# A feed-forward network in two phases: seven half products for eight in the up-projection, and a down-projection in three rounds summed in PSUM

## The chip, the cores and the metric

The kernel runs on one core of one Trainium2 chip. The metric is the device time of one execution, in microseconds, median of the runs. Matrix products run on TensorE (PE), which reads its stationary operand (128x128, the LDWEIGHTS of the profile) and its moving operand from SBUF and writes PSUM, eight banks of 128x512 fp32. VectorE (DVE), ScalarE (ACT) and GpSimd (POOL) do the elementwise work, SyncE (SP) issues most of the transfers. Each engine works through its own program in order, and the programs wait for each other by semaphores.

## The reference

One inference step of a backbone of two layers, D = 1024, over 128 context tokens and 1024 latent tokens. Each layer is a mixer (layer 0 attention and pooling, layer 1 convolution and a Fourier product), an output projection with a gated residual and LayerNorm, and then the part that changes here, the gated convolutional feed-forward network with 2816 hidden channels:

```python
def conv_ffn(u, w_up, cw, cb, w_down):
    a, g = jnp.split(u @ w_up, 2, axis=-1)
    return (jax.nn.silu(depthwise_conv(a, cw, cb)) * g) @ w_down
...
        u = layer_norm(x) * (1 + sc2) + sh2
        f = conv_ffn(u, w_up[l], ffn_conv_w[l], ffn_conv_b[l], w_down[l])
        x = layer_norm(DEEPNORM_ALPHA * x + g2 * f, ln_g[l, 1], ln_b[l, 1])
```

The convolution runs over three neighbouring tokens, for context and latent tokens apart. Context tokens are modulated and gated by their own vectors.

## The kernel before

The 1152 tokens are nine tiles of 128, tile 0 the context; three tiles make a third of 384 tokens. The 2816 hidden channels are 22 blocks of 128, in 11 groups of two. Every fp32 product is made in three passes: each operand is split into a rounded high part (a copy on ACT, line 905) and the rest, the low part (a subtraction on DVE, line 1434), and PE adds high x high, high x low and low x high.

**Start of the network.** `ln_mid` (line 2030) makes the output projection of the mixer tile by tile. For each tile DVE, POOL and ACT then normalize twice (LayerNorm with gain, then the plain one of the modulation), PE turns the tile (`ln_turn`, transposes into PSUM), ACT modulates it from PSUM and rounds it, and DVE makes its low part. The six chunks of the first hidden block (`first_chunk`) stand between the turns of tiles 6, 7 and 8; a chunk needs the tokens of its own third alone.

**Steady groups.** For a group PE runs four units (two blocks, value and gate) of three chunks (one third each) of 24 matmuls with 384 moving columns (`chunk`, line 2102), 288 in all. ACT copies the value rows out of PSUM, DVE makes the convolution, ACT the SiLU, DVE multiplies by the gate rows in PSUM and splits the product. Then come 108 down matmuls of 512 columns (`down_half`, line 2314): nine tiles, two halves of D, six matmuls each. DVE adds every 128x512 result to a sum in SBUF (line 1747). The residual gate is multiplied into the rows of w_down, twice, since the context has its own. Each weight is loaded and split once.

**End of a layer.** All nine tiles are complete only with the last group. Behind its down matmuls every tile is normalized (ACT, DVE, POOL), and in layer 0 normalized again, turned, modulated and split, with conditioning blocks (`end_block`) and the first Fourier chunks (`four_chunk`) between the turns. In layer 1 the tiles are stored.

## Time and profile before

| | |
|---|---|
| median of three runs | 2805.47 us (2804.4 to 2806.04) |
| span of the profiled execution | 2803.4 us; 2.07 us lie between it and the median of the runs |
| PE busy | 2667.1 us, 95% |
| PE weight loads busy | 2380.4 us, 85% |
| DVE, ACT, POOL busy | 1510.2, 920.3, 422.0 us |
| transfers | 196.09 MB, mean 70 GB/s |

The profile is one execution. A busy share is an average over stretches with different limits, so the views below go stretch by stretch. In a timeline, equal instructions that follow each other stand on one line with their count, and a bracket gives the idle time before the line and what ended it. PEclk is the granted clock of PE, 1.00 being full speed.

### The profile page before, as it was taken

Reading aid. Unit: us, or ns where it says so; the run is one execution under the profiler, and the core shown is the slowest. Engines: PE = TensorE matmul, PEld = TensorE weight load, DVE = VectorE, ACT = ScalarE, POOL = GpSimd, SP = SyncE. Lnnn points to the kernel's source line nnn. Section 1 sums busy time; section 2 is a strip of 40 time slices with the busy share of each in tenths; the row PEclk is TensorE's granted clock in tenths of the full one; section 3 lists DMA queues with packets and bytes.
Section 4 is the critical chain, followed back from the end, with each engine's and each line's share of the span. In section 5 each row is a group of like instructions: output and inputs, shape, how many; then the busy total and the mean of one; then the engine's idle time right before and its main releaser. Section 6 shows DMA issues by size and latency. Waiting matters only on the chain.

```text
span 2803.4 us, 36152 instructions
## 1 busy us (share of the span) xinstructions
PE 2667.1 (95%) x13884; PEld 2380.4 (85%) x13884; DVE 1510.2 (54%) x2157; ACT 920.3 (33%) x1402; POOL 422.0 (15%) x236
## 2 busy tenths in 40 slices
PE   5799899998999999999997999999999999999997
PEld 2487688687999999999995999978899999999995
DVE  2236677656555555555557433356555555555557
ACT  4412677645221222222226411136222222222213
POOL 1060587433000000000007000024000000000003
PEclk7889999999999999999999999999999999999999
DMA  9911100213111111111116212132311111111112
GB/s 330 336 38 36 31 1 1 69 69 136 45 45 37 45 45 39 43 45 45 45 34 257 63 46 67 53 105 87 109 45 45 45 45 45 45 37 40 35 31 83
DMA packets 170992, 196.09 MB, mean 70 GB/s; under 512 B 7098, under 2 KB 125350, under 8 KB 170912
## 3 DMA queue, kind: packets, MB, share of 16 engines
q1 hardware_dynamic: 169844, 194.43, 21.2%
q8 instruction: 53, 0.87, 0.1%
q10 hardware_dynamic: 491, 0.42, 0.1%
q14 instruction: 28, 0.22, 0.0%
q0 software_dynamic: 576, 0.15, 0.0%
HBM read 175.64 MB, written 19.33 MB: 70 GB/s over the span
## 4 chain that ended last, share of the span: by engine, by line
PE 83%; DVE 6%; ACT 4%; issue 3%; DMA 2%; POOL 1%; SPq 0%; ACTq 0%; POOLq 0%; DVEq 0%
PE ps L2106 48%; PE ps L2321 18%; PE ps L2073 5%; DVE small L1634 2%; DMA ada_w<-in_w_ada 2%; PE ps L2056 1%; PE ps L2154 1%; ACT p_exp L1144 1%; PE ps L2212 1%; PE ps L2233 1%; DVE stats L1464 1%; ACT ps L1305 1%; PE ps L2234 1%; PE ps L2018 1%; PE ps L2255 1%
## 5 line engine op out<-in xcount | busy, mean ns | idle before, releaser
L2106 PE MATMUL ps<-act_b,uw 128*128 128x384 f32 x4608 | 807.5, 338 | 8.9 <-DVE act_b L1434 7.4
L2106 PEld LDWEIGHTS ps<-act_b,uw 128*128 128x128 f32 x4608 | 803.6, 189 | 10.7 <-DVE act_b L1434 8.0
L2106 PEld LDWEIGHTS ps<-act_a,uw 128*128 128x128 f32 x3456 | 605.3, 190 | 14.2 <-issue 5.9
L2106 PE MATMUL ps<-act_a,uw 128*128 128x384 f32 x3456 | 610.2, 339 | 6.8 <-DVE act_a L1434 5.3
L2321 PE MATMUL ps<-dw,hh 128*128 128x512 f32 x2112 | 501.4, 397 | 9.1 <-DVE acc L1747 9.1
L2321 PEld LDWEIGHTS ps<-dw,hh 128*128 128x128 f32 x2112 | 397.2, 189 | 111.6 <-DVE acc L1747 9.9
L1747 DVE TENSOR_TENSOR acc<-acc,ps 128x512 f32<-128x512 f32 x360 | 245.8, 686 | 216.7 <-PE ps L2321 216.7
L905 ACT ACTIVATE fa<-ps 128x384 f32<-128x384 f32 (+2 forms) x176 | 67.3, 410 | 839.2 <-PE ps L2106 839.2
L1708 DVE TENSOR_SCALAR ft<-fa,fgrp 128x1153 f32<-128x1153 f32 x44 | 38.7, 880 | 299.0 <-ACT fa L905 284.1
L1434 DVE TENSOR_TENSOR uw<-raw_u,uw 128x1024 fp32r<-128x1024 f32 x112 | 136.6, 1221 | 86.3 <-ACT uw L905 83.0
L849 POOL TENSOR_TENSOR p_low<-p_exp,p_top 128x1536 fp32r<-128x1536 f32 (+1 forms) x50 | 170.9, 3420 | 71.2 <-ACT p_top L905 70.2
L1777 DVE TENSOR_TENSOR fh<-ft,ps 128x384 f32<-128x384 f32 (+2 forms) x176 | 73.9, 450 | 168.4 <-PE ps L2106 160.8
L888 POOL TENSOR_TENSOR acc<-acc,gb_end 128x1024 f32<-128x1024 f32 x9 | 21.3, 2376 | 821.8 <-ACT acc L1285 821.8
L905 ACT ACTIVATE uw<-raw_u 128x1024 fp32r<-128x1024 f32 x112 | 117.8, 1054 | 68.5 <-PE ps L2106 66.2
L905 ACT ACTIVATE hh<-fh 128x384 fp32r<-128x384 f32 x132 | 66.5, 520 | 205.6 <-DVE fh L1777 205.6
L881 POOL TENSOR_SCALAR acc<-acc,stats 128x1024 f32<-128x1024 f32 x9 | 10.8, 1199 | 806.6 <-DVE stats L1472 806.6
L862 POOL TENSOR_TENSOR ln_y<-ln_y,gbm 128x1024 f32<-128x1024 f32 x18 | 43.5, 2417 | 422.9 <-ACT ln_y L985 422.9
L1634 DVE TENSOR_REDUCE small<-ps 128x1 f32<-128x1152 f32 (+1 forms) x72 | 88.7, 1232 | 25.0 <-PE ps L2212 24.3
L1264 ACT ACTIVATE ft<-ft 128x1153 f32<-128x1153 f32 x44 | 51.5, 1171 | 132.7 <-DVE ft L1710 126.8
L1144 ACT ACTIVATE p_exp<-ps 128x1536 f32<-128x1536 f32 (+1 forms) x50 | 71.0, 1421 | 39.4 <-PE ps L2234 39.3
L1639 DVE RECIPROCAL o_inv<-o_raw 64x128 f32<-64x128 f32 x72 | 67.1, 939 | 29.7 <-ACT o_raw L905 28.9
L1434 DVE TENSOR_TENSOR hh<-fh,hh 128x384 fp32r<-128x384 f32 x132 | 73.2, 555 | 17.4 <-ACT hh L905 12.0
(215 smaller groups left out, 3094.2 us busy)
## 6 DMA issues: line engine op xcount, KB each, us to landing
raw_u<-in_w_up SPq DMA_DIRECT2D x88, 512.0 KB, 4.0
ada_w<-in_w_ada SPq DMA_DIRECT2D x52, 512.0 KB, 6.5
raw_d<-in_w_down SPq DMA_DIRECT2D x44, 512.0 KB, 3.7
end_w<-in_w_ada SPq DMA_DIRECT2D x24, 512.0 KB, 7.3
late_w<-in_w_ada SPq DMA_DIRECT2D x20, 512.0 KB, 7.0
raw_u<-in_w_in_odd SPq DMA_DIRECT2D x20, 512.0 KB, 3.9
ln_y<-in_x_all SPq DMA_DIRECT2D x18, 512.0 KB, 4.6
xs<-ln_y SPq DMA_DIRECT2D x18, 512.0 KB, 2.6
```

The lines of the kernel that those rows point to most:

```text
L849: gp.tensor_tensor(p_low[:, s % 3, 0:nb, :], p_exp[:, s % 2, 0:nb, :], p_top[:, s % 3, 0:nb, :].bitcast(F32), ALU.subtract).then_inc(p_lo, 1)
L905: return act.activation(o, i, ACT.Copy)
L1144: act.activation(p_exp[:, s % 2, 0:nb, :], ps[:, 3:3 + nb, :], ACT.Exp).then_inc(exp_done, 1)
L1264: act.activation(ft[:, 1:PADW - 2], ft[:, 1:PADW - 2], ACT.Silu).then_inc(silu_done, 1)
L1434: return v.tensor_tensor(dst, src, hi.bitcast(F32), ALU.subtract)
L1634: v.tensor_reduce(g.peak(h), ps[:, 0:nb, 0:nw], mybir.AxisListType.XY, ALU.max, negate=True).then_inc(mx_done, 1)
L1639: v.reciprocal(o_inv[g.out, cols_], o_raw[g.sum, cols_]).then_inc(inv_done, 1)
L1747: return v.tensor_tensor(a, a, ps[:, 6 + j % 2, :], ALU.add).then_inc(down_added, 1)
L1777: o = v.tensor_tensor(f_h[l][:, s0:s0 + ln], f_t[l][:, p0:p0 + ln], ps[:, 3 + c, s0 - c * CH:s0 - c * CH + ln], ALU.mult)
L2073: mm = pe.matmul(ps[:, 2 * (tile % 3) + h, :], src[:, k, a, tile * P:(tile + 1) * P], wo[l][:, k, w, 512 * h:512 * (h + 1)], start=(k, a, ...
L2106: mm = pe.matmul(out, uw[:, u_slot, w, k, :], src[:, k, a, c * CH:(c + 1) * CH], start=(k, w, a) == (0, 0, 0), stop=(k, w, a) == (KD - 1, ...
L2321: mm = pe.matmul(ps[:, 6 + h, :], hh[l][:, b, a, tile * P:(tile + 1) * P], w_[:, b, w, 512 * h:512 * (h + 1)], start=(b, a, w) == (0, 0, 0 ...
```

## The change

The network of a layer is done in two phases, with the hidden rows kept in DRAM between them.

*Up phase.* The value and the gate rows of a block, over the tokens of the first two thirds and both halves of D, are a product of 2x2 half matrices. It is made from seven half products instead of eight: with weight halves A11, A12 (value) and A21, A22 (gate), DVE forms the sums S1 to S4, and with the tokens of thirds 0 and 1 it forms three sums (`t_ops`) in `split` of tiles 3 to 5. A half product is 12 matmuls of 384 columns. The last third is plain, 48 matmuls. So a block has 132 matmuls instead of 144. Products 2, 3 and 4 are accumulated in PSUM onto 1, 5 and 7, once ACT or DVE has read what these hold; DVE forms the sums (U2, U3, G2, C12, G1) from which the convolution and the gate go on. The high part of a weight or token sum is copied by ACT and its low part made by DVE, ahead of the block that uses it. SP stores the 128x1152 hidden rows of each block.

*Down phase.* Three rounds of three tiles. In a round all 22 rows of w_down (512 KB each) and the matching hidden slices (196 KB) are loaded again and split; each row is 18 matmuls of 512 columns, summed over the 22 rows in PSUM, two banks per tile (`TILE_BANKS`). The last two rows of a round (four in the last) run tile by tile. Splits run ahead of PE by a ring of 3 (first round) or 4. DVE's evacuation of a finished tile (gate, residual), the normalizations, and in layer 0 the turns, modulations and splits of the next layer's tokens are written into the next round, between the splits of its rows j, at the places `run_down` shows. POOL does gain and bias and stores by its own queue. The gate products 3 and 4 move from `ln_mid` to rows 8 and 11 of the first round. After the last round of layer 0 only tiles 6 to 8 are left, beside the Fourier chunks.

*First block.* PE's order there is `first`: product 1, product 5, turn 6, products 7 and 6, turn 7, products 2, 4, 3, turn 8, the plain third. What ACT and DVE do for it stands in `behind(s)`, called between the normalization steps of the last tiles.

Constants and names:

```diff
-END_BANKS = (0, 2, 0, 2, 0, 6, 2, 6, 2)
+B_A, B_D, B_E, B_B, B_F, B_H = range(6)
+KH = KD // 2
+HW = KH * P
+ORDER = ("A11", "A12", "A22", "S2", "S3", "S1", "S4", "A21")
+ORDER0 = ("A11", "A12", "S3", "S1", "S2", "A22", "S4", "A21")
+NI = 3 * NF
+RAWS, RING0, RING1 = 3, 3, 4
+TILE_BANKS = ((6, 7), (0, 1), (2, 3), (4, 5), (6, 7), (0, 1), (2, 3), (4, 5), (6, 7))
+TURN_BANKS = ((2, 3),) * 3 + ((0, 1),) * 6
+FOUR_BANKS = ((2, 3, 4), (5, 6, 7))
+FOUR_ORDER = ((0, 0), (0, 1), (1, 0), (1, 1), (0, 2), (1, 2))
+END_SPOTS = {39: 0, 60: 1}
+END_BANKS = (2, 0, 4, 7, 4, 7)
+LAST_ROWS = 4
```

SyncE:

```diff
+                def down(self, i):
+                    l, (r, f) = self.l, divmod(i, NF)
+                    if i >= RAWS:
+                        sp.wait_ge(dn_lo, NI * l + i - RAWS + 1)
+                    if r == 0:
+                        sp.wait_ge(h_st[f % 2], 16 * (NG * l + f // 2 + 1))
+                    sp.dma_start(d_raw_of(l, i)[:], dram_rows(t["w_down"][l], f)).then_inc(w_ld[i % RAWS], 16)
+                    sp.dma_start(h_raw[i % RAWS][:], h_rows[l][f * P:(f + 1) * P, r * CH:(r + 1) * CH]).then_inc(w_ld[i % RAWS], 16)
...
+                def run_down(self, beside=lambda i: None):
+                    l = self.l
+                    sp.wait_ge(w_lo, 8 * NF * (l + 1))
+                    for i in range(RAWS):
+                        self.down(i)
+                    self.store(NG - 1, 0)
+                    self.store(NG - 1, 1)
+                    sp.wait_ge(p_h, NF * (l + 1))
+                    gate_rows(l, e_z[l], 5)
+                    for c, row in enumerate((t["ln_g"], t["ln_b"])):
+                        sp.dma_start(gb_end[l][:, c, :], row[l, 1, :].partition_broadcast(P)).then_inc(gb_ld, 16)
+                    self.rows(0)
+                    for i in range(RAWS, NI):
+                        if i in (NF + 18, 2 * NF + 15):
+                            self.rows(i // NF)
+                        beside(i)
+                        self.down(i)
 
```

ScalarE:

```diff
+                def rounding(tile):
+                    sl = slice(tile * P, (tile + 1) * P)
+                    act.wait_ge(mod_done, tile + (NT * i4 + 1))
+                    if 3 <= tile < 6:
+                        copy(dest[:, KH:KD, 0, sl], halves(ln_u[:, tile, HW:D]))
+                        act.wait_ge(t_sum, 4 * l + tile - 2)
+                        copy(dest[:, 0:KH, 0, sl], halves(ln_u[:, tile - 3, 0:HW])).then_inc(act_hi, 1)
+                        return
+                    copy(dest[:, :, 0, sl].rearrange("p (a k) t -> p a k t", a=2), token_tile(tile).rearrange("p a (k t) -> p a k t", t=P)).then_inc(act_hi, 1)
...
+                def behind(self, s):
+
+                    l = self.l
+                    if s == NT - 1:
+                        self.turned(0)
+                        self.turned(1)
+                        act.wait_ge(out_evac, NT * (l + 1))
+                        self.hi(0, 0, "S2")
+                        self.hi(0, 0, "A22")
+                    elif s == NT:
+                        self.turned(2)
+                        self.first_product(0, 0)
+                        act.wait_ge(t_lo, 3 * (l + 1))
+                        self.hi(0, 0, "S4")
+                        self.hi(0, 0, "A21")
+                    elif s == NT + 1:
+                        self.first(0, 0)
+                        act.wait_ge(act_rdy, NT * (2 * l + 2))
+                        for slot in range(3):
+                            act.wait_ge(x_st[slot], 48 * (l + 1))
+                        for x in ORDER[:6]:
+                            self.hi(0, 1, x)
+                        self.third(0, 0)
+                        self.hi(0, 1, "S4")
+                        self.silu(0, 0)
...
+                def run_down(self, beside):
+                    self.hi(NG - 1, 1, "A21")
+                    for i in range(NI):
+                        self.down(i)
+                        if i == RING0 - 1:
+                            self.block(NG - 1, 1, True)
+                        r, j = divmod(i, NF)
+                        if i in (12, 14):
+                            self.gate(3 + (i - 12) // 2)
+                        if r and j in (3, 4, 5):
+                            self.norm1(3 * (r - 1) + j - 3)
+                        if r and self.l == 0:
+                            if j in (9, 12, 15):
+                                self.modulate(3 * (r - 1) + j // 3 - 3)
+                            if j in (6, 9, 12):
+                                self.norm2(3 * (r - 1) + j // 3 - 2)
```

VectorE:

```diff
+                def split(tile):
+                    sl = slice(tile * P, (tile + 1) * P)
+                    if 3 <= tile < 6:
+                        before, here = ln_u[:, tile - 3, :], ln_u[:, tile, :]
+                        v.wait_ge(mod_done, tile + (NT * i4 + 1))
+                        v.tensor_tensor(before[:, 0:HW], here[:, 0:HW], before[:, 0:HW], ALU.subtract).then_inc(t_sum, 1)
+                        v.tensor_tensor(here[:, 0:HW], here[:, HW:D], here[:, 0:HW], ALU.subtract)
+                        v.wait_ge(act_hi, tile + (NT * i4 + 1))
+                        v.wait_ge(t_sum, 4 * l + tile - 2)
+                        lo(dest[:, KH:KD, 1, sl], halves(here[:, HW:D]), dest[:, KH:KD, 0, sl])
+                        lo(dest[:, 0:KH, 1, sl], halves(before[:, 0:HW]), dest[:, 0:KH, 0, sl]).then_inc(act_rdy, 1)
+                        chain(v.tensor_tensor(here[:, HW:D], here[:, HW:D], before[:, 0:HW], ALU.subtract))
+                        o = v.tensor_tensor(before[:, HW:D], before[:, HW:D], here[:, HW:D], ALU.subtract)
+                        if tile == 5:
+                            o.then_inc(t_sum, 1)
+                        return
...
+                def sums(self, g, b):
+                    base = NF * self.l + b
+                    a11, a12, a21, a22 = (operand(x, False, b) for x in ("A11", "A12", "A21", "A22"))
+                    s1, s2, s3, s4 = (operand(x, False, b) for x in ("S1", "S2", "S3", "S4"))
+                    v.wait_ge(w_lo, total(g, 16, 8 * base + 3))
+                    chain(v.tensor_tensor(s1, a21, a22, ALU.add))
+                    chain(v.tensor_tensor(s2, s1, a11, ALU.subtract))
+                    v.tensor_tensor(s3, a11, a21, ALU.subtract)
+                    v.tensor_tensor(s4, a12, s2, ALU.subtract).then_inc(comb_rdy, 1)
+
...
+                def gate2(self, g, b):
+                    l, n = self.l, NF * self.l + b + 1
+                    v.wait_ge(p_d, total(g, 4, 2 * n - 1))
+                    v.wait_ge(summed, sums_until(l, g, b, "U3"))
+                    v.tensor_tensor(f_v[l][:], f_v[l][:], ps[:, B_D, 0:CH], ALU.add).then_inc(summed, 1)
...
+                def behind(self, s):
+
+                    if s == NT - 1:
+                        self.turned(0)
+                        self.turned(1)
+                        self.late_sums()
+                        self.lo(0, 0, "S2")
+                        self.lo(0, 0, "A22")
+                    elif s == NT:
+                        self.turned(2)
+                        self.second(0, 0)
+                        self.third(0, 0)
+                        self.gate2(0, 0)
+                        self.lo(0, 0, "S4")
+                        self.lo(0, 0, "A21")
...
+                def evac(self, tile):
+                    l, slot = self.l, tile % 3
+                    x, y = banks(TILE_BANKS[tile]), e_y[l][:, slot, :].rearrange("p (a n) -> p a n", a=2)
+                    v.wait_ge(dn_done, NT * l + tile + 1)
+                    v.wait_ge(gate_rdy, 4 * l + 4)
+                    chain(v.tensor_tensor(x, x, g_end[l][1 if tile == 0 else 0][:].rearrange("p (a n) -> p a n", a=2), ALU.mult))
+                    v.wait_ge(x_ld[slot], 48 * (2 * l + 2) + 16 * (tile // 3 + 1))
+                    v.scalar_tensor_tensor(y, y, ALPHA, x, ALU.mult, ALU.add).then_inc(dn_evac, 1)
...
+                def run_down(self, beside=lambda i: None):
+                    self.lo(NG - 1, 1, "A21")
+                    for i in range(NI):
+                        self.down(i)
+                        if i == RING0 - 1:
+                            self.block(NG - 1, 1, True)
+                        r, j = divmod(i, NF)
+                        if r:
+                            t0 = 3 * (r - 1)
+                            if j == 2:
+                                self.evac(t0)
+                                self.evac(t0 + 1)
+                            elif j == 3:
+                                self.evac(t0 + 2)
+                            if j in (3, 4, 5):
+                                self.stats1(t0 + j - 3)
+                            if self.l == 0:
+                                if j in (9, 12, 15):
+                                    self.split(t0 + j // 3 - 3)
+                                if j in (6, 9, 12):
+                                    self.stats2(t0 + j // 3 - 2)
+                        beside(i)
```

TensorE:

```diff
+                def p3(self, w, n):
+                    g, b = n
+                    pe.wait_ge(summed, sums_until(self.l, g, b, "G2"))
+                    self.product(B_D, w["S4"], self.block_x(1, 1), False, True, p_d)
...
+                def first(self, turn):
+
+                    l, n, w = self.l, (0, 0), w_ops[0]
+                    rows, out = NT * (2 * l + 1), NT * l
+                    self.operands(0, 0, 4)
+                    pe.wait_ge(act_rdy, rows + 3)
+                    pe.wait_ge(out_evac, out + 7)
+                    self.p1(w)
+                    pe.wait_ge(act_rdy, rows + 6)
+                    self.p5(w)
+                    turn(6)
+                    pe.wait_ge(out_evac, out + 8)
+                    pe.wait_ge(t_lo, 3 * l + 1)
+                    self.p7(w)
+                    pe.wait_ge(t_lo, 3 * l + 2)
+                    self.operands(0, 0, 5)
+                    self.p6(w)
+                    turn(7)
+                    self.p2(w, n)
+                    pe.wait_ge(t_lo, 3 * l + 3)
+                    self.operands(0, 0, 6)
+                    self.p4(w, n)
+                    self.operands(0, 0, 7)
+                    self.p3(w, n)
+                    turn(8)
+                    pe.wait_ge(act_rdy, rows + 9)
+                    pe.wait_ge(out_evac, out + 9)
+                    self.plain(B_F, w["A11"], w["A12"], p_f)
+                    self.operands(0, 0, 8)
+                    self.plain(B_H, w["A21"], w["A22"], p_h)
+
...
+                def block(self, g, b):
+                    n, w = (g, b), w_ops[b]
+                    before = NF * self.l + b
+
+                    def free(s):
+                        pe.wait_ge(s, total(g, 2, before))
+
+                    self.operands(g, b, 2)
+                    free(a2_ev)
+                    self.plain(B_F, w["A11"], w["A12"], p_f)
+                    free(a_ev)
+                    self.p1(w)
+                    self.operands(g, b, 4)
+                    pe.wait_ge(summed, sums_until(self.l, g, b - 1, "U2"))
+                    self.p6(w)
+                    self.operands(g, b, 5)
+                    pe.wait_ge(summed, sums_until(self.l, g, b - 1, "G1"))
+                    self.p7(w)
+                    self.operands(g, b, 6)
+                    pe.wait_ge(summed, sums_until(self.l, g, b - 1, "C12"))
+                    self.p5(w)
+                    self.p2(w, n)
+                    self.operands(g, b, 7)
+                    self.p3(w, n)
+                    self.p4(w, n)
+                    self.operands(g, b, 8)
+                    free(h_mul)
+                    self.plain(B_H, w["A21"], w["A22"], p_h)
...
+                def down(self, i, tile):
+                    f, d, h = i % NF, d_split_of(i), h_split[self.l][i % RING1]
+                    for half in range(2):
+                        out = ps[:, TILE_BANKS[tile][half], :]
+                        for a, w in PASSES:
+                            mm = pe.matmul(out, h[:, a, tile % 3 * P:(tile % 3 + 1) * P], d[:, w, 512 * half:512 * half + 512],
+                                           start=f == 0 and (a, w) == (0, 0), stop=f == NF - 1 and (a, w) == (1, 0))
+                    return mm
...
+                def run_down(self, beside=lambda i: None):
+                    for r in range(3):
+                        rows = LAST_ROWS if r == 2 else 2
+                        for f in range(NF - rows):
+                            i = r * NF + f
+                            if i in (8, 11):
+                                self.gate(3 + (i - 8) // 3)
+                            beside(i)
+                            pe.wait_ge(dn_lo, NI * self.l + i + 1)
+                            for tile in range(3 * r, 3 * r + 3):
+                                if f == 0:
+                                    self.rows_free(tile)
+                                mm = self.down(i, tile)
...
+            def end_beside(i):
+                if i in (30, 33, 36):
+                    end_turn((30, 33, 36).index(i))
+                elif i in (52, 55, 58):
+                    end_turn(3 + (52, 55, 58).index(i))
+                elif i in END_SPOTS:
+                    end_block(END_SPOTS[i])
...
+            four_chunk(0, 0)
+            end_turn(6)
+            four_chunk(0, 1)
+            end_block(2)
+            end_turn(7)
+            four_chunk(1, 0)
+            four_chunk(1, 1)
+            end_block(3)
+            end_turn(8)
+            end_block(4)
             end_block(5)
```

## Rows read from the trace of the kernel before

**Rows 1.** The page, parts 1 and 4: busy shares; chain by line.

```profile
PE 2667.1 (95%) x13884; PEld 2380.4 (85%) x13884; DVE 1510.2 (54%) x2157; ACT 920.3 (33%) x1402; POOL 422.0 (15%) x236
...
PE ps L2106 48%; PE ps L2321 18%; PE ps L2073 5%; DVE small L1634 2%; DMA ada_w<-in_w_ada 2%; PE ps L2056 1%; PE ps L2154 1%; ACT p_exp L1144 1%; PE ps L2212 1%; PE ps L2233 1%; DVE stats L1464 1%; ACT ps L1305 1%; PE ps L2234 1%; PE ps L2018 1%; PE ps L2255 1%
```

**Rows 2.** Windows of one group: us, busy per engine, PEclk, DMA share, GB/s.

```profile
741.71:791.63 49.92, 49.92 (x289) 49.92 (x289) 26.88 (x31) 14.92 (x22) 0.00 (x0) 1.00 0.22 64
791.63:816.83 25.20, 25.20 (x110) 20.32 (x109) 13.16 (x20) 1.58 (x2) 0.00 (x0) 1.00 0.00 1
```

**Rows 3.** Timeline of PE at the start of layer 0's network.

```profile
652.15 4.33 PE L2106 MATMUL ps<-act_b,uw 128*128 128x384 f32 x24
...
672.13 1.09 PE L2018 MATMUL ps<-con,ln_z 128*128 128x128 f32 x8 [1.41 <-ACT ln_z L1004]
678.56 11.19 PE L2106 MATMUL ps<-act_b,uw 128*128 128x384 f32 x48 [5.33 <-DVE act_b L1434]
691.19 25.24 PE L2106 MATMUL ps<-act_b,uw 128*128 128x384 f32 x144 [1.45 <-DVE uw L1434]
```

**Rows 4.** Windows of 4 us in that stretch (columns as in Rows 2).

```profile
672.00:676.00 4.00, 1.09 (x8) 0.85 (x8) 0.21 (x1) 2.82 (x9) 0.00 (x0) 0.75 0.89 326
676.00:680.00 4.00, 1.44 (x4) 1.44 (x5) 1.31 (x2) 2.03 (x5) 0.00 (x0) 0.50 1.01 407
```

**Rows 5.** Lines by form: xcount | busy us, mean ns | idle before, releaser.

```profile
L1747 DVE TENSOR_TENSOR acc<-acc,ps 128x512 f32<-128x512 f32 x360 | 245.8, 686 | 216.7 <-PE ps L2321 216.7
...
L1434 DVE TENSOR_TENSOR uw<-raw_u,uw 128x1024 fp32r<-128x1024 f32 x112 | 136.6, 1221 | 86.3 <-ACT uw L905 83.0
...
L1434 DVE TENSOR_TENSOR hh<-fh,hh 128x384 fp32r<-128x384 f32 x132 | 73.2, 555 | 17.4 <-ACT hh L905 12.0
...
L905 ACT ACTIVATE hh<-fh 128x384 fp32r<-128x384 f32 x132 | 66.5, 520 | 205.6 <-DVE fh L1777 205.6
...
L862 POOL TENSOR_TENSOR ln_y<-ln_y,gbm 128x1024 f32<-128x1024 f32 x18 | 43.5, 2417 | 422.9 <-ACT ln_y L985 422.9
```

**Rows 6.** Timeline of DVE in the stretch of Rows 3.

```profile
653.45 1.83 DVE L1434 TENSOR_TENSOR act_b<-ln_u,act_b 128x1024 f32 x1 [0.76 <-ACT act_b L905]
...
668.08 1.29 DVE L1464 BATCH_NORM_STATS2 stats<-ln_y 128x6 f32<-128x512 f32 x2 [2.29 <-POOL ln_y L864]
...
670.03 0.17 DVE L1471 RECIPROCAL stats<-stats 128x1 f32<-128x1 f32 x1 [0.36 <-ACT stats L989]
...
677.28 1.23 DVE L1434 TENSOR_TENSOR act_b<-ln_u,act_b 128x1024 fp32r<-128x1024 f32 x1 [5.07 <-ACT act_b L905]
```

**Rows 7.** Timeline of ACT in the stretch of Rows 3.

```profile
670.85 1.22 ACT L1004 ACTIVATE ln_z<-ln_y,stats 128x1024 f32<-128x1024 f32 x1
673.26 2.90 ACT L976 ACTIVATE ln_u<-ps,cols 128x128 f32<-128x128 f32 x8 [1.18 <-PE ps L2018]
676.19 1.06 ACT L905 ACTIVATE act_b<-ln_u 128x1024 fp32r<-128x1024 f32 x1
```

**Rows 8.** DMA issues: xcount, KB each, median us to landing.

```profile
raw_d<-in_w_down SPq DMA_DIRECT2D x44, 512.0 KB, 3.7
...
acc<-xs SPq DMA_DIRECT2D x6, 1536.0 KB, 12.0
```

**Rows 9.** Timeline of PE from layer 0's last group to the Fourier products.

```profile
1467.55 2.95 PE L2321 MATMUL ps<-dw_ctx,hh 128*128 128x512 f32 x12
...
1494.01 1.04 PE L2354 MATMUL ps<-con,raw_d 128*128 128x128 f32 x8
1494.98 1.93 PE L2366 MATMUL ps<-end_w,conds 128*32 128x512 f32 x16
...
1570.87 11.35 PE L2416 MATMUL ps<-chan,f_in 128*128 128x256 f32 x78 [0.27 <-DVE cols L1459]
1583.63 1.55 PE L2429 MATMUL ps<-ctab,f_ch 128*128 128x128 f32 x12 [1.41 <-DVE f_ch L1434]
```

**Rows 10.** Window of the end of layer 1 (columns as in Rows 2).

```profile
2754.84:2803.00 48.16, 28.23 (x109) 20.53 (x107) 39.30 (x84) 15.67 (x21) 21.34 (x9) 0.87 0.24 98
```

More of the change, by code:

```diff
@@ L1848, in tab_lo @@
+            f.stats2(7)
+            f.split(7)
+            f.stats2(8)
+            f.split(8)
             def tab_lo(k):
```

1279 lines of the change are left out of this document (712 added, 567 removed).

## The prediction

> **What bounds the kernel now.** I read the page's shares first, then the chain that ended last, then the stretches around each feed-forward network. TensorE (PE) is busy 95% of the 2803.4 us span, and two thirds of the last chain are its up-projection and down-projection lines [rows 1]. [rows 2] is one inner group: 49.92 us for 288 up matmuls without a gap, 0.1733 each, then 25.20 for 108 down matmuls, 0.2333 each, at granted clock 1.00 (2.4 GHz). There PE is the limit and VectorE (DVE) and ScalarE (ACT) have half their time free. So a matmul removed is worth its 0.1733 us, if what feeds PE keeps up. [rows 3] is the opposite stretch, the start of the network: the 48 matmuls at 678.56 take 11.19 us against 8.32 at the steady pace, behind waits of 1.41, 5.33 and 1.45. There a chain of short ACT, DVE and PE steps is the limit, and the clock follows: 0.75 and 0.50 (0.50 is 1.2 GHz) in the two stretches where PE mostly waits [rows 4]. The change is worth its matmuls in the steady blocks and costs what it adds to such chains. All sums are against the profiled 2803.4; the median of the runs, 2805.47, is 2.07 above it, and I add 2.07 at the end.
>
> **a. Fewer up matmuls.** Per hidden block 8 products of 12 matmuls for two thirds of the tokens become 7: 132 for 144. 44 blocks x 12 x 0.1733 [rows 2] = **-91.5 us**. The new feeding work fits: a steady block is 132 x 0.1733 = 22.9 us of PE, and the tightest wait in it is on the sum that product 3 needs. PE reaches it 84 matmuls into the block, at 14.56; DVE makes it by adding product 5 (done after 72 matmuls, 12.48) in one 128x384 instruction, 0.55 [rows 5], plus a hop: 13.3, so 1.2 us to spare. DVE gains four weight sums and a third more splits, but loses the 18 additions of 0.69 per group [rows 5].
>
> **b. The first block.** Today its chunks need only the tokens of one third each. After, product 5 needs tiles 3 to 5 in their new form, and products 7, 6 and 4 need sums over tiles 0 to 5, before turns 7 and 8 in PE's order; and what serves these stands in ACT's and DVE's queues ahead of the normalization of the last tiles. I follow layer 0 from the same projection end, 652. Tile 5 takes six half-size DVE instructions instead of one; beside GpSimd (POOL) a 128x1024 split takes 1.83, not 1.23 [rows 6], so it is ready at 660.4, not 655.3; product 5 and turn 6 end at 663.5. Then one after another: ACT's modulate 2.9 and rounding 1.05 [rows 7], DVE's statistics 1.7 with their root's hop of 0.36 and scale [rows 6], ACT's normalize 1.22 [rows 7]: 671.6. Behind that ACT copies the first sum, 128x1536, 1.5 by the 1.05 for 1024 [rows 7], and DVE makes its low part, 1.8: product 7 starts at 674.9. A second sum 1.8, the weight sums 1.4 and a split 1.3: product 6 at 679.5, and turn 7 behind it ends at 683.5. Modulate, root, rounding, normalize, the third sum's copy 1.5 and product 1's copy 0.5: product 2 at 691.0. Products 2, 4 and 3 are 36 matmuls, 6.2, plus 2.8 for the half clock (what the 48 of [rows 3] lost), so 700, turn 8 at 701. Modulate, rounding and split 5.2: 706.3; the last 48 matmuls 8.3 + 2.9: **717.5**. Today the second block starts at 691.19 [rows 3]. With 12 matmuls fewer in the first it should start 2.1 earlier, and it starts 26.3 later: 28.4 per layer, **+56.8**. From both sides: 0 if all of it hides as well as today; +40 per layer if the half clock reaches all 132 matmuls.
>
> **c. From up to down.** Row 3 of the down phase waits for its load, which SyncE issues behind the h stores, the broadcast rows and three residual rows, 3.1 MB. At the 326 GB/s of [rows 4] that is 9.5, plus 3.7 to land [rows 8] and 3.4 to split; PE has three rows of 18 x 0.2333 = 4.2 in hand: 4 late, **+8** for two layers. Below: 0, if row 3 overtakes them; above: at 1536 KB in 12.0 [rows 8], 3.1 MB take 24, 18 late.
>
> **d. Changes of round.** The down matmuls are as many as now, and accumulating in PSUM removes no PE time. But at the end E of a round, the evacuation of its first tiles stands on DVE behind the split of the round's third new row, and that waits for a ring slot that PE frees only 1.4 before E. So evacuations of 1.22 + 1.22 each (as 128x1024 in [rows 5]) end at E+4.6 and E+7.1, while PE wants the banks at E+1.4 and one tile (1.4) later: PE waits **4.35**. Then three rows carry a tile's first normalization between splits, all in one chain: ACT 1.5 (1.05 + 0.52), DVE 1.8 (1.22 + 0.55) [rows 5, 7], statistics 1.65, root 0.35, scale 0.45, normalize 1.22 [rows 6, 7] = 6.9 per row against PE's 4.2. The ring holds four rows; the third such split is ready at E+32.15 and PE wants it at E+29.5: **2.65** late. Layer 0 has three more rows with second normalizations (one late by 2.65 again) and turns: modulate, rounding, split, statistics, normalize and two splits, 13.1 against two rows and a turn in hand, 9.2, late 3.9 twice. So 17.45 per round in layer 0, 7.0 in layer 1, two rounds each: 48.9. POOL's affine beside these lengthens DVE: I add 2.5 per round, for four or five instructions 0.6 longer. **+59**. Bounds: 17.4, the four bank waits alone; 90, if every DVE instruction of these rows is half as long again.
>
> The Trainium skill, "SBUF — State Buffer", Who interferes with whom, says that a two-input DVE instruction with both inputs in SBUF contends with a GpSimd instruction that reads SBUF, and that the shared pair is locked, not throttled. The row shows 1.83 for 1.23 beside POOL [rows 6]: 0.6 lost, not a whole POOL addition of 2.42 [rows 5]. By the rule taken at its word the wait is up to a POOL instruction each, which is rival 3.
>
> **e. End of layer 0.** Today from the last group's down matmuls to the first Fourier product: 1570.87 - 1467.55 - 25.2 = 78.1 us [rows 9]. After, only three tiles are left at T, the end of round 2: tile 6 normalized twice 14.7 (with a 1.93 conditioning block before it), then per tile turn, modulate, rounding, normalize about 5: turn 8 at 35.3, ACT busy until 40.7, modulate and split to 45.9, two chunks 8.3, fold and split 7.7: 61.9. Six turns of 0.8 and two conditioning blocks of 1.93 [rows 9] move into rounds: 8.7. 70.6 - 78.1 = **-7.5** (bounds -19, if the Fourier chunks fill all waits, and +5).
>
> **f. End of layer 1.** Today 2803.4 - 2754.84 - 25.2 = 23.4 [rows 10]: nine tiles' normalizations trail. After, three: evacuation 2.4, statistics to normalize 3.7, affine on DVE 2.4, a 512 KB store by the 3.7 of a load [rows 8], the last tile some 3 later: 15.2. **-8.2**.
>
> **Sum.** -91.5 + 56.8 + 8 + 59 - 7.5 - 8.2 = **+16.6**: span 2820.0, **2822 us** in the runs.
>
> **Rivals.**
> 1. *The hops hide.* I put the steps of b and d end to end; queues may overlap them, since DVE and ACT are half idle in the mean, and the rows of today's start lose only 11 us to it [rows 3]. With 12 per layer for b and 30 for d: -91.5 + 24 + 8 + 30 - 15.7 = -45: **2760**, faster. It decides when all added waits stay under 107 (91.5 + 15.7). Against it: the order of the queues is fixed, and PE itself stands between the steps. Chance 0.25.
> 2. *PE is all that counts.* All of a comes off and nothing is given back: **2714**. Chance 0.05. The Trainium skill, "Perfetto Trace Analysis", Identifying the Most-Contended Engine, has one find the engine with most contention and improve it, which here is PE by [rows 1]; [rows 3] shows the stretches where that doesn't hold.
> 3. *POOL locks DVE out.* Six POOL instructions of 2.4 per round stop DVE in full, 14.4 for my 2.5, four rounds: +48, **2870**. Against: [rows 6]. Chance 0.06.
> 4. *Product 3's sum is late in every block.* The spare 1.2 us is a hop or two; if DVE is held by a weight split for 2.2, 1 us x 44: **2866**, slower. Chance 0.08.
> 5. *Loads bound the down rows.* 708 KB per 4.2 us is 169 GB/s; with 3 buffers, landing 3.7 and the split it is (3.7 + 4)/3 = 2.6 per row, hidden. With 10 to land, (10 + 3.7)/3 = 4.6: 132 rows x 0.4 = +50: **2872**. Chance 0.06.
> 6. *It doesn't give the products.* The sums of tokens move as three pieces of 128 columns. No such row is there; as three matmuls of 128 (1.55 / 12 = 0.129 each [rows 9]) they would add 0.214 x 36 x 44 = 339: **3161**. As likely it costs nothing, since the columns are the same. Chance 0.03.
>
> **Chances and range.** My forecast has 0.47; its own range is 2795 to 2850, from the bounds of b and d. What a measurement can tell from no change is 0.2%, 5.6 us: 2799.9 to 2811.1. Faster: most of rival 1, rival 2, and a little of the forecast's low end: 0.29. Same: 0.12. Slower: 0.59. For 8 in 10, I leave out rival 2, the lower part of rival 1, rival 6 and half of 3 to 5: **2745 to 2870**.
>
> **What would show it.** Up blocks at 22.9 us with no wait in the steady part (a); the first block's end 26 us later, with turn 7 near 683 and half clock around it (b); idle PE before the second and third tile of each round, 4.35 together, then at rows 6, and in layer 0 rows 7, 10 and 13 of a round (d). I am wrong if the start and the rounds give back less than 107 us together, or if a steady block shows a wait.

## The result and the profile after

| | before | after |
|---|---|---|
| median of the runs | 2805.76 us (4 runs) | 2893.76 us (4 runs, 2888.34 to 2899.64) |
| span of the profiled execution | 2803.4 | 2891.1 |
| ratio | | 1.0315, 95% interval 1.0299 to 1.0331 |

The change makes the kernel 88 us slower. The forecast was 2822, its range ended at 2870: the sign was right, the size was not. From the page of the changed kernel, parts 1 and 5, and last the row of the down matmuls on the page of the kernel before:

```profile
PE 2619.4 (91%) x13356; PEld 2317.4 (80%) x13356; DVE 1660.6 (57%) x2446; ACT 1086.0 (38%) x1730; POOL 434.7 (15%) x245
...
L2769 PE MATMUL ps<-d_ring,hs 128*128 128x512 f32 x2376 | 588.0, 408 | 76.8 <-DVE hs L1639 62.9
...
L2321 PE MATMUL ps<-dw,hh 128*128 128x512 f32 x2112 | 501.4, 397 | 9.1 <-DVE acc L1747 9.1
```

PE is busy 48 us less than in [rows 1], yet the span is 88 longer. Ahead of the down matmuls alone PE waits 76.8 us, 62.9 of it for DVE's split of a hidden slice; before, the same kind of line waited 9.1. By stage, in us (letters as in the prediction):

| step of the prediction | forecast | measured |
|---|---|---|
| a. up matmuls | -91.5 | -91.5 |
| b. first block | +56.8 | +60.2 |
| c. up to down, first round | +8 | +27.8 |
| d. changes of round | +59 | +93.4 |
| e. end of layer 0 | -7.5 | +6.2 |
| f. end of layer 1 | -8.2 | -7.8 |
| sum | +16.6 | +88.3 (the spans: +87.7) |

The rows behind the table, PE first (start, us, x matmuls, idle before): the first block of layer 0, then steady blocks of layer 1.

```profile
661.50 4.21 PE L2628 MATMUL ps<-act_b,w_S 128*128 128x384 f32 x12 [7.86 <-DVE act_b L1639]
...
679.75 4.18 PE L2628 MATMUL ps<-t,w_S 128*128 128x384 f32 x12 [12.33 <-DVE t L1639]
...
694.62 4.04 PE L2628 MATMUL ps<-act_b,w_A 128*128 128x384 f32 x12 [7.01 <-ACT fp L1002]
...
709.04 16.17 PE L2628 MATMUL ps<-act_b,w_A 128*128 128x384 f32 x84 [5.35 <-DVE act_b L1639]
725.05 4.32 PE L2628 MATMUL ps<-t,w_S 128*128 128x384 f32 x24
...
2078.40 4.32 PE L2628 MATMUL ps<-t,w_S 128*128 128x384 f32 x24
...
2101.28 4.32 PE L2628 MATMUL ps<-t,w_S 128*128 128x384 f32 x24
```

The same place of two blocks lies 22.88 us apart: 132 matmuls at 0.1733, no wait, for 24.96 before; over 44 blocks that is the 91.5 of a. The sums of tokens (`t`), which move in three pieces, take 4.32 for 24 like any other, so rival 6 is out. The second block of layer 0 begins 36 matmuls ahead of 725.05, at 718.8; in [rows 3] at 691.19. In layer 1, from the first Fourier product to the second block: 435.9 after, 407.5 before. So 27.6 + 28.4, and 2.1 each for the 12 matmuls less: 60.2.

PE in the first two rounds of layer 0:

```profile
1220.08 22.94 PE L2769 MATMUL ps<-d_ring,hs 128*128 128x512 f32 x90 [5.91 <-DVE hs L1639]
...
1306.27 1.62 PE L2769 MATMUL ps<-d_ring,hs 128*128 128x512 f32 x6 [0.30 <-PE ps L2769]
1310.31 1.66 PE L2769 MATMUL ps<-d_ring,hs 128*128 128x512 f32 x6 [2.42 <-DVE ey L2100]
1312.71 18.38 PE L2769 MATMUL ps<-d_ring,hs 128*128 128x512 f32 x78 [0.73 <-DVE ey L2100]
1336.30 6.15 PE L2769 MATMUL ps<-d_ring,hs 128*128 128x512 f32 x18 [5.21 <-DVE hs L1639]
1346.04 6.00 PE L2769 MATMUL ps<-d_ring,hs 128*128 128x512 f32 x18 [3.59 <-DVE hs L1639]
1352.68 4.45 PE L2769 MATMUL ps<-d_ring,hs 128*128 128x512 f32 x18 [0.65 <-DVE hs L1639]
...
1370.07 6.00 PE L2769 MATMUL ps<-d_ring,hs 128*128 128x512 f32 x18 [3.70 <-DVE hs L1639]
```

Row 3 of the down phase waits 5.91, 4.83 in layer 1 (c, which is counted from the place where the last up block should end to the start of the second round, less 92.4: 14.6 and 13.2). In the change of round the bank waits are 0.30, 2.42 and 0.73. Then two rows with a normalization come 9.74 apart (1336.30 to 1346.04), not 6.9, and rows that come late are slow too: 6.0 to 6.15 for their 18 matmuls here, up to 7.0 further on, instead of 4.45. The windows of the four later rounds, and of one such late row (columns as in Rows 2):

```profile
1306.27:1432.81 126.54, 106.14 (x437) 82.21 (x437) 67.77 (x90) 53.83 (x86) 18.70 (x9) 0.92 0.53 184
1432.81:1560.58 127.77, 106.57 (x437) 82.00 (x437) 73.88 (x97) 51.57 (x82) 23.72 (x11) 0.92 0.43 148
2658.24:2767.06 108.82, 96.48 (x397) 76.56 (x397) 58.99 (x69) 37.81 (x52) 18.65 (x9) 0.97 0.52 175
2767.06:2875.54 108.48, 96.67 (x396) 76.65 (x396) 64.89 (x81) 34.55 (x48) 18.64 (x9) 0.95 0.41 142
...
1336.30:1342.30 6.00, 6.00 (x18) 4.57 (x18) 2.89 (x7) 2.91 (x4) 2.84 (x2) 0.69 0.76 251
```

Each round has 92.4 us of matmuls; in layer 0 4.3 of turns and a conditioning block come to it. What is left is 29.8, 31.1, 16.4 and 16.1: 93.4. The late row had a granted clock of 0.69. DVE, then POOL, in those rows:

```profile
1321.62 2.24 DVE L1639 TENSOR_TENSOR d_ring<-d_raw,d_ring 128x1024 fp32r<-128x1024 f32 x1 [2.68 <-ACT hs L1002]
1323.78 2.76 DVE L1639 TENSOR_TENSOR hs<-h_raw,hs 128x384 fp32r<-128x384 f32 x1
```

```profile
1320.37 2.40 POOL L981 TENSOR_TENSOR ey<-ey,gb_end 128x1024 f32<-128x1024 f32 x1 [642.15 <-ACT ey L1458]
1322.85 3.27 POOL L983 TENSOR_TENSOR ey<-ey,gb_end 128x1024 f32<-128x1024 f32 x1
```

This is the heart of it. A split that alone takes 1.22 takes 2.24, and one of 0.55 takes 2.76. The first ends 1.1 after POOL's first addition has ended (1322.77), the second 0.4 after POOL's second (1326.12); and that one takes 3.27 instead of 2.40, being held by the first split in turn. Whichever of the two comes second waits until the other has ended, and then takes its usual time.

The end of layer 0:

```profile
1560.58 4.40 PE L2416 MATMUL ps<-act_b,uw 128*128 128x384 f32 x24 [0.30 <-PE ps L2769]
...
1588.08 1.97 PE L2809 MATMUL ps<-con,ez 128*128 128x128 f32 x8 [12.11 <-ACT ez L1467]
...
1606.02 1.74 PE L2825 MATMUL ps<-end_w,conds 128*32 128x512 f32 x8 [3.53 <-DMA end_w<-in_w_ada]
...
1636.25 11.33 PE L2884 MATMUL ps<-chan,f_in 128*128 128x256 f32 x78 [0.27 <-DVE cols L1664]
```

From the last round to the Fourier product 75.7 us pass (forecast 61.9); with the 8.6 of turns and blocks that went into the rounds that is 6.2 more than the 78.1 of before. Turn 7 waits 12.1, and the last two conditioning blocks wait 8.0 in four pieces for loads. Layer 1 ends 15.6 after its last matmul, before 23.4.

### The profile page after: what moved, and what is told of

It reads as the page before. It is cut to its first block and busy times, and to the rows that moved or that the text cites. A ratio compares the mean times of both kernels' runs of the same rounds, so it can differ in the third digit from the quotient of the medians.

```text
span 2891.1 us, 35791 instructions
## 1 busy us (share of the span) xinstructions
PE 2619.4 (91%) x13356; PEld 2317.4 (80%) x13356; DVE 1660.6 (57%) x2446; ACT 1086.0 (38%) x1730; POOL 434.7 (15%) x245
## 5 line engine op out<-in xcount | busy, mean ns | idle before, releaser
L2769 PE MATMUL ps<-d_ring,hs 128*128 128x512 f32 x2376 | 588.0, 408 | 76.8 <-DVE hs L1639 62.9
L2769 PEld LDWEIGHTS ps<-d_ring,hs 128*128 128x128 f32 x2376 | 462.0, 196 | 201.9 <-DVE hs L1639 70.8
L2628 PE MATMUL ps<-act_a,w_A 128*128 128x384 f32 x1584 | 286.5, 340 | 13.6 <-ACT fp L1002 8.3
L2628 PE MATMUL ps<-act_b,w_A 128*128 128x384 f32 x1584 | 285.2, 339 | 13.5 <-ACT fp L1002 8.1
L2628 PEld LDWEIGHTS ps<-act_a,w_A 128*128 128x128 f32 x1584 | 279.4, 191 | 14.5 <-ACT fp L1002 8.8
L2628 PEld LDWEIGHTS ps<-act_b,w_A 128*128 128x128 f32 x1584 | 278.1, 190 | 14.3 <-ACT fp L1002 8.7
L2416 PEld LDWEIGHTS ps<-act_b,uw 128*128 128x128 f32 x1440 | 253.2, 191 | 2.4 <-issue 2.4
L2416 PE MATMUL ps<-act_b,uw 128*128 128x384 f32 x1440 | 254.6, 340 | 0.3 <-PE ps L2769 0.3
L2628 PE MATMUL ps<-t,w_S 128*128 128x384 f32 x1056 | 194.8, 341 | 25.2 <-DVE t L1639 24.7
L2628 PEld LDWEIGHTS ps<-t,w_S 128*128 128x128 f32 x1056 | 187.0, 191 | 26.7 <-issue 26.7
```

The lines of the kernel that those rows point to most:

```text
L2416: mm = pe.matmul(out, uw[:, u_slot, w, k, :], src[:, k, a, c * CH:(c + 1) * CH], start=(k, w, a) == (0, 0, 0), stop=(k, w, a) == (KD - 1, ...
L2628: mm = pe.matmul(o, w[:, a, k, :], m, start=first and (k, a, i) == (0, 0, 0), stop=last and (k, a, i) == (KH - 1, 1, 0), skip_group_check= ...
L2769: mm = pe.matmul(out, h[:, a, tile % 3 * P:(tile % 3 + 1) * P], d[:, w, 512 * half:512 * half + 512], start=f == 0 and (a, w) == (0, 0), s ...
```

## The experiments

All are edits of the changed kernel; times are to be held against its 2893.8. Runs 1 to 10 are one execution each. Executions of the changed kernel itself lie up to 11 us apart, so a difference of a few us between two times shows nothing by itself, and the traces have to say where it lies.

**1. Gain and bias left out on POOL.**

```diff
-                    gp.tensor_tensor(y, y, gb_end[l][:, 0, :], ALU.mult).then_inc(g_mul, 1)
+                    gp.tensor_tensor(y[:, 0:1], y[:, 0:1], gb_end[l][:, 0, 0:1], ALU.mult).then_inc(g_mul, 1)
...
-                    gp.tensor_tensor(y, y, gb_end[l][:, 1, :], ALU.add).then_inc(x1_rdy, 1)
+                    gp.tensor_tensor(y[:, 0:1], y[:, 0:1], gb_end[l][:, 1, 0:1], ALU.add).then_inc(x1_rdy, 1)
```

> Leaves out the gain and bias of the end LayerNorm on POOL for all columns but one (two additions of 128x1024 become two of 128x1). Theory 1: the rows of a round that carry a normalization are 9.7 us apart and not the 6.9 of the forecast because POOL's two 2.4 us instructions stop the DVE splits beside them (2.2 + 2.7 us for 1.22 + 0.55). Then these splits go back to 1.22 and 0.55, the rows come 6.9 apart, a round after the first loses about 11 us in layer 0 (126.7 now) and 9 in layer 1 (109 now), and the whole about 40: 2854. Theory 2: the chain of ACT, DVE and hops is itself longer than was summed, POOL only runs beside it: spacing stays over 9, time stays within 8 us of 2894.

Measured: 2853.97. DVE and PE in the same rows, then the windows of the four later rounds (columns as in Rows 2):

```profile
1325.06 1.22 DVE L1639 TENSOR_TENSOR d_ring<-d_raw,d_ring 128x1024 fp32r<-128x1024 f32 x1 [2.67 <-ACT hs L1002]
1326.21 0.55 DVE L1639 TENSOR_TENSOR hs<-h_raw,hs 128x384 fp32r<-128x384 f32 x1
```

```profile
1333.45 4.45 PE L2769 MATMUL ps<-d_ring,hs 128*128 128x512 f32 x18 [1.36 <-DVE hs L1639]
1340.09 6.00 PE L2769 MATMUL ps<-d_ring,hs 128*128 128x512 f32 x18 [2.19 <-DVE hs L1639]
```

```profile
1303.08:1423.13 120.05, 105.59 (x437) 81.92 (x437) 58.42 (x90) 53.77 (x86) 2.93 (x9) 0.93 0.56 194
1423.13:1544.13 121.00, 105.75 (x437) 81.57 (x437) 64.53 (x99) 51.33 (x82) 3.77 (x12) 0.93 0.46 161
2640.95:2739.09 98.14, 94.46 (x397) 75.20 (x397) 49.66 (x69) 37.74 (x52) 2.86 (x9) 0.98 0.56 194
2739.09:2836.65 97.56, 94.55 (x396) 75.15 (x396) 55.58 (x81) 34.39 (x48) 2.82 (x9) 0.98 0.46 158
```

The splits have their short times back and the rows are 6.64 apart, near the 6.9 of the forecast. Theory 1 holds: POOL holds DVE within the chain. The four rounds take 436.75 together, 34.9 less than the 471.61 above, and that is what POOL cost there. Of the other 5 us of the 40, some 2 lie at the end of layer 0; 3 lie ahead of the first of these rounds (it starts at 1303.08 and not 1306.27), where the edit changes nothing. POOL's own time in the way of the next step is no rival: in layer 1 its result is only stored, and the rounds there become 10.7 and 10.9 shorter.

**2. Two memsets on POOL instead.**

```diff
+                    gp.memset(y, 0.5).then_inc(g_mul, 1)
...
+                    gp.memset(y, 0.25).then_inc(x1_rdy, 1)
```

> Gain and bias are replaced by two memsets of 128x1024 on POOL at the same places: POOL is busy and writes SBUF, but reads none (the end LayerNorm's output is lost). If it is POOL's reads that stop a DVE instruction with two SBUF inputs, as the Trainium skill has it (SBUF — State Buffer, Who interferes with whom), the splits beside a memset take 1.22 and 0.55 and the time is as without the additions, about 2854. If any POOL access to SBUF stops DVE, the splits beside a memset are lengthened by what is left of it, and the time lies between 2854 and 2894.

Measured: 2858.07. POOL's second memset and the split that runs beside it:

```profile
1322.83 0.95 POOL L983 MEMSET ey<- 128x1024 f32 x1
```

```profile
1323.10 1.23 DVE L1639 TENSOR_TENSOR d_ring<-d_raw,d_ring 128x1024 fp32r<-128x1024 f32 x1 [2.67 <-ACT hs L1002]
```

They overlap for 0.68 us and the split is not lengthened. A memset is shorter than an addition, so this is an overlap of two thirds of a microsecond and not of a whole instruction, but it speaks for reads as what counts. The 4.1 us to run 1 are too few to read anything from.

**3. Turns ahead of products in the first block.** Turn 7 directly behind turn 6, turn 8 ahead of product 2.

```diff
                     turn(6)
+                    turn(7)
...
                     self.p6(w)
-                    turn(7)
+                    turn(8)
                     self.p2(w, n)
...
                     self.p3(w, n)
-                    turn(8)
```

> In PE's order of the first block turn 7 stands directly behind turn 6 (ahead of products 7 and 6), and turn 8 ahead of product 2. Theory 1 (what the forecast of the start rests on: the hops stand end to end because PE's order puts products between the turns): the modulation of tile 7 starts 7 us earlier and the second block some 17 us earlier in each layer, time 2894 - 34 = 2860. Theory 2: the sums over tiles 0 to 5 on DVE set the end whatever the order of the turns: the second block starts within 4 us of where it does now, time 2886 to 2894.

Measured: 2866.46. PE:

```profile
688.19 1.31 PE L2341 MATMUL ps<-con,ln_z 128*128 128x128 f32 x8 [2.42 <-ACT ln_z L1105]
...
697.68 14.83 PE L2628 MATMUL ps<-act_b,w_A 128*128 128x384 f32 x84
712.35 4.32 PE L2628 MATMUL ps<-t,w_S 128*128 128x384 f32 x24
```

The second block comes 12.7 us earlier (712.35 for 725.05). Theory 1, somewhat less than its 17: turn 8, at 688.19, now waits 2.42 for its own normalization; how much of the missing 4 that is was not followed.

**4. Loads of rows 3 to 5 early.**

```diff
                     self.store(NG - 1, 0)
+                    for i in range(RAWS, 2 * RAWS):
+                        self.down(i)
                     self.store(NG - 1, 1)
```

> SyncE issues the loads of rows 3 to 5 of the down phase ahead of the store of the last hidden block, for which it waits 21 us, and so ahead of the broadcast rows and the three residual rows. Theory 1: row 3 is late because its load stands behind that wait and 3.1 MB: the wait of 5.9 us (layer 0) and 4.8 (layer 1) before row 3 goes, and 2 us of lower clock behind each: 2894 - 14 = 2880. Theory 2: the queue only moves the delay to row 6, which then comes as late as row 3 did: no change beyond 3 us.

Measured: 2880.47. PE runs the first eight rows without a wait:

```profile
1205.47 33.77 PE L2771 MATMUL ps<-d_ring,hs 128*128 128x512 f32 x144
```

Theory 1. In the changed kernel row 3's load stood in SyncE's queue behind 21.0 us of waiting for the last hidden rows and was issued at 1206.47, 5.1 after the down phase had begun, with the 3.1 MB in front of it. The run takes both away, and so does not tell them apart.

**5. Evacuations one row earlier.**

```diff
-                            if j == 2:
+                            if j == 1:
                                 self.evac(t0)
                                 self.evac(t0 + 1)
-                            elif j == 3:
+                            elif j == 2:
                                 self.evac(t0 + 2)
```

> DVE's evacuations of a finished round's first two tiles stand behind the split of the next round's second row instead of its third, the last tile's behind the third instead of the fourth. Theory 1 (the forecast's: PE waits for banks because the evacuation stands behind a split that waits for a ring slot): the waits of 0.3, 2.4 and 0.7 us before the first row's tiles go in all four changes of round, and the normalizations start that much earlier: 4 x 3.4 to 5 us, 2874 to 2880. Theory 2: what PE gains there it loses at the rows with normalizations, whose splits come no earlier: no change beyond 4 us.

Measured: 2874.05. Theory 1. The first late row keeps a wait of 4.09, where it was 5.21.

**6. Order at the end of layer 0.** ACT's `end_evac(2)` moves behind `norm2(7)`; PE runs block 3 ahead of the Fourier chunks (1, 0) and (1, 1), and block 4 ahead of turn 8.

```diff
             four_in(0, 0)
-            end_evac(2)
             f.norm1(8)
             f.modulate(6)
             f.norm2(7)
+            end_evac(2)
...
             end_turn(7)
+            end_block(3)
             four_chunk(1, 0)
             four_chunk(1, 1)
-            end_block(3)
+            end_block(4)
             end_turn(8)
-            end_block(4)
             end_block(5)
```

> End of layer 0, order alone: ACT takes conditioning block 2 out of PSUM behind tile 6's modulation and tile 7's normalization instead of ahead of them; PE runs block 3 ahead of the two Fourier chunks and block 4 ahead of turn 8, so that the loads of the next block (four slots, each block's four loads wait for the block before) run beside other work. Theory 1: the 75.7 us from the end of the last round to the first Fourier product hold 12.1 of waiting for tile 7, of which about 7 is ACT behind that block, and 8.0 for the blocks' loads: 60 to 63 remain, time 2878 to 2881. Theory 2: tile 8's own chain of normalization, turn and split sets the end: no change beyond 4 us.

Measured: 2883.2, less of a gain than theory 1 has it: turn 7 waits 5.67 instead of 12.11, the blocks' loads still cost 4.3 of the 8.0.

**7. Gain and bias on DVE, in the old chain.**

```diff
+                            if j in (4, 5, 6):
+                                self.affine(t0 + j - 4)
                             if j in (3, 4, 5):
                                 self.stats1(t0 + j - 3)
```

> Of the new rounds only the gain and bias on DVE: each tile's two additions of 1.22 us stand behind the split of the row after its normalization, in the chain of the changed kernel; POOL only stores. If the lengthened splits (3.1 us a row) were a cost of POOL's work that goes as soon as POOL is idle, about 2854 as without the additions. If what counts is that the steps stand in one chain, DVE's 2.4 us take the place of the 3.1: rows 9.1 apart instead of 9.7, time 2884 to 2894.

Measured: 2884.43. The late rows come 9.0 apart. That POOL is idle gives only some 9 us, and not the 40 of run 1, when DVE does the work at the same place.

**8. New rounds.** Gain and bias on DVE, evacuations early, and each step in a row of its own behind the one it waits for. Layer 1 in full, layer 0 in part (number: row of the round; last digit: tile):

```diff
+DVE_PLAN = (
+    {1: "evac0 evac1", 2: "stats1a0 evac2 scale1_0", 3: "stats1a1", 4: "affine0 stats2a0", 5: "scale1_1 stats1a2", 6: "scale2_0 scale1_2", 7: "affine1", 8: "stats2a1",
...
+    {1: "evac0 evac1", 2: "evac2", 3: "stats1a0 scale1_0", 4: "affine0", 6: "stats1a1 scale1_1", 7: "affine1", 9: "stats1a2 scale1_2", 10: "affine2"})
+ACT_PLAN = (
+    {2: "root1_0", 3: "norm1_0", 5: "root1_1", 6: "norm1_1", 7: "root2_0 root1_2 z0", 8: "norm1_2 mod0", 9: "root2_1", 10: "round0", 11: "z1 root2_2", 12: "z2 mod1", 13: "round1",
...
+    {3: "root1_0 norm1_0", 6: "root1_1 norm1_1", 9: "root1_2 norm1_2"})
+TURN_ROWS = (6, 9, 13)
```

> Changes of round written anew: gain and bias on DVE (POOL only stores), evacuations one row earlier, and statistics, root, scale, normalization, turn and modulation each in a row of its own, a row or more behind the step it waits for, so that no split stands behind a round trip between ACT and DVE. Theory 1: the rounds cost 126.6 (layer 0) and 109 us (layer 1) for 92.4 of matmuls because of the order of these steps and POOL beside them, not because ACT or DVE have too much to do: a round then takes 97 to 99 us in layer 0 (turns and a block are 4.3 of it) and 93 to 94 in layer 1, together -88: 2806. Theory 2: DVE has too little time left in these rows once it makes gain and bias too (7.3 us a round): rounds stay above 105 and 98, time above 2835.

Measured: 2800.34. Theory 1, with 93 us gained: no late row is left.

**9. New rounds, gain and bias on POOL again** (the plan without its `affine` entries).

> The new rounds with gain and bias left on POOL, where they were: evacuations one row earlier and the steps spread over rows of their own, but DVE's splits still meet POOL's two instructions per tile. If the order is what counts, the splits beside POOL still take 2.2 + 2.7 us and yet no row is late in layer 1, since three rows lie between two normalizations: rounds of 93 to 95 us in layer 1 and under 104 in layer 0, time below 2825. If the lock itself has to go, each tile still costs its 3.1 us: rounds of 101 to 103 in layer 1, over 108 in layer 0, time above 2835.

Measured: 2805.18. PE's two later rounds of layer 1, the windows of those of layer 0 (columns as in Rows 2), and a split beside POOL in layer 1:

```profile
2603.02 92.27 PE L2797 MATMUL ps<-d_ring,hs 128*128 128x512 f32 x396 [0.30 <-PE ps L2797]
2695.59 92.28 PE L2797 MATMUL ps<-d_ring,hs 128*128 128x512 f32 x396 [0.30 <-PE ps L2797]
```

```profile
1309.49:1406.99 97.50, 97.09 (x437) 77.22 (x437) 64.74 (x89) 52.71 (x85) 18.84 (x9) 1.00 0.67 239
1406.99:1504.93 97.94, 97.57 (x437) 77.12 (x437) 68.63 (x94) 50.74 (x82) 24.38 (x11) 1.00 0.56 193
```

```profile
2615.72 2.76 DVE L1665 TENSOR_TENSOR hs<-h_raw,hs 128x384 fp32r<-128x384 f32 x1
```

The order is what counts. The split still takes 2.76, and the round is 92.6 us long, without a wait for it. In layer 0 the rounds take 97.50 and 97.94, where they took 97.33 and 98.03 in run 8 without POOL's work. So the 4.8 us between the two runs do not lie in the rounds.

**10. All of it:** the new rounds (gain and bias on DVE), early loads, the end of layer 0, the turns of run 3, and in the first block also turn 6 ahead of product 5.

> The new rounds, the loads of rows 3 to 5 early, the new order at the end of layer 0, and in the first block turn 6 ahead of product 5, turn 7 behind it and turn 8 ahead of product 2. If the losses are separate and stand end to end, the gains add up: -88 (rounds), -13 (loads), -14 (end of layer 0), -27 and about -7 (start): 2745, 2% faster than the kernel before. If one loss hides another, the sum is less: between 2760 and 2790.

Measured: 2749.5. PE in the first six rows of a round of layer 0, up to its first turn, and in the two later rounds of layer 1:

```profile
1285.76 25.33 PE L2800 MATMUL ps<-d_ring,hs 128*128 128x512 f32 x108 [0.30 <-PE ps L2800]
...
2548.25 92.26 PE L2800 MATMUL ps<-d_ring,hs 128*128 128x512 f32 x396 [0.30 <-PE ps L2800]
2640.81 92.28 PE L2800 MATMUL ps<-d_ring,hs 128*128 128x512 f32 x396 [0.30 <-PE ps L2800]
```

The losses stood end to end and their cures add up: runs 3, 4, 6 and 8 gain 27.3, 13.3, 10.6 and 93.4, 144.6 in sum, and this one 144.3. Timed:

> The kernel with all four reorderings, timed against the kernel before: 2749 to 2752, a ratio of 0.980 to 0.982. If the one look at it was a lucky run, the interval reaches above 0.985.

Measured: 2747.52 (five runs, 2745.16 to 2750.78) against 2805.66 for the kernel before: ratio 0.9796, interval 0.9782 to 0.9809. The same arithmetic as in the changed kernel, put in another order and with gain and bias on DVE, is 146 us faster than it and 58 faster than the kernel before.

## Why the prediction was wrong

**a, b and f held, b with some luck.** The 91.5 us of a were there. The chain of b, followed hop by hop, gave the second block at 717.5 and the trace 718.8. On the way the trace is as much as 4.9 later than the working (product 7 at 679.75 for 674.9): product 5 and turn 6 were counted at full speed and ran at a granted clock of 0.50. It comes back in part because the last 48 matmuls take 9.8 and not 11.2. Run 3 shows where much of the loss comes from: PE's own order put products between the turns.

**d failed, and it is the largest part of the error: 93.4 for 59, 34 us of the 72 by which the sum was off.** The step was "POOL's affine beside these lengthens DVE: I add 2.5 per round, for four or five instructions 0.6 longer". The 0.6 was read off [rows 6] as a slowdown by half. It was what was left of a POOL instruction. POOL in that stretch of the kernel before:

```profile
651.76 2.43 POOL L862 TENSOR_TENSOR ln_y<-ln_y,gbm 128x1024 f32<-128x1024 f32 x1 [6.53 <-ACT ln_y L985]
654.27 3.26 POOL L864 TENSOR_TENSOR ln_y<-ln_y,gbm 128x1024 f32<-128x1024 f32 x1
```

POOL ends its first addition at 654.19; the split of [rows 6] starts at 653.45, waits 0.74, and ends 1.1 after. POOL's second takes 3.26 for the same work. The lock could be read from the trace of before, by setting the start of the long instruction beside the end of the other engine's. The Trainium skill, "SBUF — State Buffer", Who interferes with whom, says just this (a two-input DVE instruction contends with GpSimd's reads, and the pair is locked and not throttled), and here trace and page agree. So rival 3's mechanism was the case, and it was given 0.06. It priced the lock at 14.4 a round, 58 for the four; by run 1 it cost 34.9 there, and the forecast had 10. Without POOL's work the rounds of run 1 still lose 58.5 (436.75 less the matmuls, turns and blocks), where the sum had 48.9 without POOL: the granted clock of 0.69 in rows that come late, 1.6 us a row, was counted in b and put at nothing here; against that the bank waits were 3.45 and not 4.35.

Run 9 adds what the rival did not have: in the new rounds the lock is still there and lengthens no round. It cost 34.9 us because each row's split stood in one chain with a round trip between ACT and DVE, which at 6.64 was already longer than PE's row of 4.2. In that chain what was added came out in full: rows 9.74 apart, 3.1 more, for splits lengthened by 1.0 and 2.2.

**c left out most of what it cost (27.8 for 8).** The wait for row 3 was nearly right, 5.9 and 4.8 for 4 in each layer; the sum had the 3.1 MB and not SyncE's late issue. Put at nothing were three terms. The two gate products, 2 x 1.98 on PE in the first round of each layer, were taken as moved at no price: 7.9. The 90 matmuls behind the wait take 22.94 and 22.62 for 21.0, at granted clocks of 0.91 and 0.93: 3.6. Some 2 us per layer are late sums of the last up block, which stand behind the splits of the first three down rows in ACT's and DVE's order. Run 4 got back what hangs on the load, 13 us with the slow matmuls behind it.

**e (+6.2 for -7.5).** Missed: four load slots for the blocks instead of eight, so that the last two wait 8.0 for loads, and ACT waiting 8.4 for a block before tile 7's work. Run 6 got 10.6 back by order; what eight slots would give was not run.

**The rivals.** Rival 1 (the hops hide) was out in this kernel. It was right as a possibility: the order of run 10 hides most of them, and its 2760 is near the 2749.5 measured. Rival 2 is out too, since the added waits are there. Rival 4 did not come: no steady block waits. Rival 5 did not come: loads of 512 KB land in 3.4 us.

## What to carry to other kernels

When an instruction is sometimes longer, set its start and end beside those of the other engines: if it ends its usual time after the end of one engine's instruction each time, it was waiting for that one, and the price is up to the whole of that instruction. In programs that run in order, work put between the steps of a stream costs its whole chain of round trips, and not its busy time alone, once that chain is longer than the stream's own step; give each step a row of its own, a row behind what it waits for. Here even the lock then lengthened no round. Judge a saving of arithmetic only after that: with the same saving this kernel was 88 us slower or 58 us faster than the kernel before. How much of the 58 is the saving stays open, since the kernel before was not put in a new order itself.

## What the runs showed of the hardware

A DVE instruction with one of its two inputs in PSUM was not held. DVE, then POOL, at the end of layer 0 of the changed kernel:

```profile
1556.30 2.58 DVE L1639 TENSOR_TENSOR uw<-raw_u,uw 128x1024 fp32r<-128x1024 f32 x1 [2.26 <-ACT uw L1002]
1558.81 1.22 DVE L2098 TENSOR_TENSOR ps<-ps,g_end 128x1024 f32<-128x1024 f32 x1
```

```profile
1557.88 3.26 POOL L983 TENSOR_TENSOR ey<-ey,gb_end 128x1024 f32<-128x1024 f32 x1
```

The split with two SBUF inputs takes 2.58, and the gate product with PSUM as one input runs in 1.22 in the middle of POOL's addition.
